# Token rows ahead of conditioning weights in the opening of a hybrid diffusion layer

## The reference

```python
def mixer_layer(x, mod, rms_g, w_in, b_in, ..., attend):
    shift, scale, gate = jnp.split(mod, 3, axis=-1)
    h = rmsnorm(x, rms_g) * (1 + scale) + shift
    q, k, v, z_a, glu, z_b, gates = jnp.split(h @ w_in + b_in, PROJ_SPLITS, axis=-1)
    ...
    return x + gate * (m @ w_out), k, v

mod_ctx = jax.nn.silu(c_ctx) @ w_ada[l] + b_ada[l]
mod_lat = (jax.nn.silu(c) @ w_ada[l] + b_ada[l])[:, None, :]
```

## Time and profile before

| | us |
|---|---|
| median of 3 runs | 1874.98 (1872.67 to 1877.26) |
| the profiled execution | 1877.82 |
| its span, first to last instruction | 1875.6 |
| TensorE busy | 1829.8 (98%) |
| VectorE busy | 1015.1 (54%) |
| ScalarE busy | 542.0 (29%) |
| GpSimd busy | 122.8 (7%) |

### The profile page before, as it was taken

One profiled execution on the slowest core, in us unless ns is written; L12 is line 12 of the kernel. 1 busy time (PEld: TensorE's weight loads), 2 busy tenths in 40 slices (PEclk: granted clock), 3 DMA queues, 4 the chain that ended last, 5 costly groups with the idle time before them and its releaser, 6 DMA issues.

```text
span 1875.6 us, 27263 instructions
## 1 busy us (share of the span) xinstructions
PE 1829.8 (98%) x10723; PEld 1561.1 (83%) x10723; DVE 1015.1 (54%) x1710; ACT 542.0 (29%) x1061; POOL 122.8 (7%) x205
## 2 busy tenths in 40 slices
PE   6999999999999999999999999999999899999998
PEld 3788899988888888888888888888888888888886
DVE  3544512111098338816870996766768555654444
ACT  3731101021111111211110114667768222322221
POOL 0100000000000000000000004322330000000000
PEclk9999999999999999999999999999999999999999
DMA  9524423143022112211220164997887767653321
GB/s 318 169 89 158 144 68 132 49 140 115 12 78 89 65 34 82 76 40 59 72 80 20 65 153 119 211 178 163 175 182 176 229 205 244 193 191 140 141 101 56
DMA packets 211145, 235.08 MB, mean 125 GB/s; under 512 B 47707, under 2 KB 157131, under 8 KB 207819
## 3 DMA queue, kind: packets, MB, share of 16 engines
q1 hardware_dynamic: 210760, 233.24, 42.5%
q10 hardware_dynamic: 259, 0.11, 0.0%
HBM read 152.52 MB, written 80.78 MB: 124 GB/s over the span
## 4 chain that ended last, share of the span: by engine, by line
PE 90%; SPq 4%; DMA 2%; issue 1%; ACT 1%; DVE 1%; POOLq 0%; DVEq 0%; POOL 0%; ACTq 0%
PE banks L789 17%; PE banks L790 17%; PE banks L791 17%; PE banks L1742 4%; PE banks L1741 4%; PE banks L1743 4%; PE banks L1713 3%; PE banks L1715 3%; PE banks L1714 3%; PE banks L1225 3%; SPq L1093 2%; PE banks L784 2%; PE banks L785 2%; PE banks L786 2%; PE banks L1191 2%
## 5 line engine op out<-in xcount | busy, mean ns | idle before, releaser
L789 PE MATMUL banks<-h_hi,w_hi 128*128 128x512 f32 (+1 forms) x1600 | 593.3, 371 | 3.6 <-DVE h_lo L598 2.5
L790 PE MATMUL banks<-h_lo,w_hi 128*128 128x512 f32 (+1 forms) x1600 | 589.4, 368 | 0.0
L791 PE MATMUL banks<-h_hi,w_lo 128*128 128x512 f32 (+1 forms) x1600 | 589.3, 368 | 0.0
L730 DVE SCALAR_TENSOR_TENSOR conv_acc<-glu_out,taps,conv_acc 128x773 f32<-128x773 f32 x360 | 371.5, 1032 | 12.3
L789 PEld LDWEIGHTS banks<-h_hi,w_hi 128*128 128x128 f32 x1600 | 301.8, 189 | 57.6 <-issue 3.4
L791 PEld LDWEIGHTS banks<-h_hi,w_lo 128*128 128x128 f32 x1600 | 301.8, 189 | 50.7
L790 PEld LDWEIGHTS banks<-h_lo,w_hi 128*128 128x128 f32 x1600 | 302.0, 189 | 49.0
L506 ACT ACTIVATE out_stage<-banks,param_cols 128x512 f32<-128x512 f32 (+1 forms) x120 | 77.0, 647 | 439.2 <-PE banks L791 433.2
L1713 PE MATMUL banks<-y_hi,wp_hi 128*128 128x512 f32 (+1 forms) x320 | 120.0, 375 | 4.9 <-DVE m_sum L1935 2.8
L1332 ACT ACTIVATE probs<-scores,stat 128x640 f32<-128x640 f32 (+2 forms) x128 | 106.7, 834 | 60.2 <-DVE stat L1259 58.6
L1715 PE MATMUL banks<-y_hi,wp_lo 128*128 128x512 f32 (+1 forms) x320 | 118.4, 370 | 0.0
(11 more groups left out here) (161 smaller groups left out, 2397.5 us busy)
## 6 DMA issues: line engine op xcount, KB each, us to landing
proj<-out_stage SPq DMA_DIRECT2D x96, 256.0 KB, 2.0
w_raw<-in_w_in SPq DMA_DIRECT2D x44, 512.0 KB, 3.9
gates_in<-proj SPq DMA_DIRECT2D x64, 256.0 KB, 2.9
k_hi<-k_hi_rows SPq DMA_DIRECT2D x16, 640.0 KB, 13.2
k_lo<-k_lo_rows SPq DMA_DIRECT2D x16, 640.0 KB, 15.2
w_ada<-in_w_ada SPq DMA_DIRECT2D x8, 1024.0 KB, 10.8
x_out<-in_x_sample SPq DMA_DIRECT2D x16, 512.0 KB, 3.4
out_y_sample<-x_out SPq DMA_DIRECT2D x15, 512.0 KB, 2.6
```

Source lines behind the costliest of these rows:

```text
L730: op = dve.scalar_tensor_tensor(dst, src, tap, dst, ALU.mult, ALU.add)
L789: pe.matmul(out, w_hi[:, s, k], h_hi[c][:, k], start=first, stop=False)
L790: pe.matmul(out, w_hi[:, s, k], h_lo[c][:, k], start=False, stop=False)
L791: op = pe.matmul(out, w_lo[:, s, k], h_hi[c][:, k], start=False, stop=last)
```

## The change

The rows of chunk 0 are loaded ahead of the first conditioning quarter and in two halves, each `w_in` block ahead of the next quarter, and every engine's written order up to `turn(9)` is changed. The first half of chunk 0 is signalled by `vb_in`, a semaphore that a later load uses too, whose wait becomes 32. `RMS` has one entry more, since the four tiles of chunk 0 are now two pairs.

```diff
-RMS = [(0, 0, 4), (1, 0, 2), (1, 2, 2), (2, 0, 4), (4, 0, 2), (3, 0, 4)]
+RMS = [(0, 0, 2), (0, 2, 2), (1, 0, 2), (1, 2, 2), (2, 0, 4), (4, 0, 2), (3, 0, 4)]
...
-            if c == 1:
-                sp.dma_start(xs[c][:, 0:2], src[:, 0:2]).then_inc(x_half_in, 16)
+            if c < 2:
+                sp.dma_start(xs[c][:, 0:2], src[:, 0:2]).then_inc(x_half_in[c], 16)
...
+        load_x(0)
         load_ada(0)
-        load_x(0)
+        load_w(sp, 0)
         load_ada(1)
-        load_w(sp, 0)
+        load_w(sp, 1)
         load_ada(2)
-        load_w(sp, 1)
+        load_w(sp, 2)
         load_ada(3)
-        load_w(sp, 2)
         load_x(1)
...
+        squares(0, 0)
+        squares(0, 1)
         row_of(0)
-        squares(0)
         high(0)
+        modulate(0)
+        modulate(1)
+        high(1)
         row_of(1)
-        for s in range(4):
-            modulate(s)
-        high(1)
+        modulate(2)
+        modulate(3)
+        high(2)
         row_of(2)
         modulate(4)
         modulate(5)
         row_of(3)
-        high(2)
         squares(1, 0)
         modulate(6)
         modulate(7)
...
+        normalize(0)
+        normalize(1)
         coefficients(0)
-        normalize(0)
         low(0)
+        split(0)
+        split(1)
+        low(1)
         coefficients(1)
-        for s in range(4):
-            split(s)
-        low(1)
+        split(2)
+        split(3)
+        low(2)
         coefficients(2)
         split(4)
         split(5)
-        low(2)
         coefficients(3)
...
-        ada_products(0)
         pe.wait_ge(rows_in, 16 * 7)
         pe.transpose(ps_rows, rows[0:R_C, :], cst.ident[0:R_C, 0:R_C]).then_inc(turned, 1)
         pe.transpose(ps_taps, taps[0:4 * TAPS, :], cst.ident[0:4 * TAPS, 0:4 * TAPS]).then_inc(turned, 1)
-        turn_row(0)
         pe.wait_ge(cols_out, 2)
-        ada_products(1)
         for s in range(3):
             turn(s)
-        turn_row(1)
+        ada_products(0)
+        turn_row(0)
         step(0, [0])
         turn(3)
         step(1, [0])
         turn(4)
+        ada_products(1)
+        turn_row(1)
+        step(0, [1])
+        step(1, [1])
         step(2, [0])
         turn(5)
         step(3, [0])
+        turn(6)
+        step(2, [1])
+        step(3, [1])
         ada_products(2)
-        for s in range(4):
-            step(s, [1])
+        for s in range(3):
+            step(s, [2])
         turn_row(2)
+        step(3, [2])
+        step(4, [0])
+        turn(7)
+        step(4, [1])
         ada_products(3)
-        turn(6)
-        step(4, [0, 1])
+        step(4, [2])
         turn_row(3)
-        turn(7)
-        step(5, [0, 1])
-        for s in range(6):
-            step(s, [2])
+        step(5, [0])
+        turn(8)
+        step(5, [1, 2])
         step(6, [0, 1])
-        turn(8)
+        turn(9)
         step(6, [2])
-        turn(9)
         step(7, [0, 1])
```

More of the change, by code:

```diff
@@ L248, in modulation @@
     ident_in, rows_in, c_in, x_in = sem("ident_in"), sem("rows_in"), sem("c_in"), [sem(f"x_in{c}") for c in range(5)]
-    x_half_in, wide_set = sem("x_half_in"), sem("wide_set")
+    wide_set = sem("wide_set")
     ada_in, gate_in, gb_in, vb_in = [sem(f"weights_in{i}") for i in range(8)], sem("gate_in"), [sem("gate_bias_in0"), sem("gate_bias_in1")], sem("vb_in")
+    x_half_in = [vb_in, sem("x_half_in")]
     tab_zero, tab_in, tab_out = sem("tab_zero"), sem("tab_in"), sem("tab_out")
@@ L447, in squares @@
         def squares(c, half=None):
-            act.wait_ge(x_half_in if half == 0 else x_in[c], 16)
+            act.wait_ge(x_half_in[c] if half == 0 else x_in[c], 16)
             for t in range(CHUNKS[c][1] // P) if half is None else range(2 * half, 2 * half + 2):
@@ L614, in front_dve @@
         split(7)
-        normalize(1)
         normalize(2)
+        normalize(3)
         s = KC
@@ L624, in front_dve @@
             if i == 10:
-                normalize(3)
+                normalize(4)
             if i == 16:
-                normalize(4)
+                normalize(5)
             if i == 19:
-                normalize(5)
+                normalize(6)
         pending = []
@@ L659, in front_dve @@
                 if n == 7 and c == 0:
-                    dve.wait_ge(vb_in, 16)
+                    dve.wait_ge(vb_in, 32)
                 s = slot_of[u]
```

## The result

The changed kernel takes 1890.6 us, median of four runs (1889.6 to 1891.7), before 1875.8 beside them: a ratio of 1.0081 (95% interval 1.0064 to 1.0099), 14.8 us slower. The forecast was 1887, in a range of 1882 to 1892.

A forecast was written before the change was run, and what follows sets the result against it. TensorE was taken as the bound, so an opening shift carries to the end: -4.6 + 2.7 + 3.5 + 7.0 + 3.4 = +12.0 us on the median of 1875.0, forecast 1887 us, range 1882 to 1892.

The forecast's parts named there:

- T0: Start of TensorE's first triple (three products of one k step, one column block): forecast at 26.7 us, 4.6 us earlier.
- (b): TensorE: quarter 1's products and folding, formerly ahead of the first triple, now stand behind its start: +2.7 us.
- (e): TensorE's clock: three restarts at half speed after idle time against one before: +3.4 us, bounds 0 and +6.
- (c): TensorE waits for coefficients around quarter 1's folding, step 2 and step 4: 0.71, 1.04 and 1.73 us, sum +3.5.
- (d): Chunk 1's first turn on TensorE waits 7.2 us, as ScalarE's squares stand behind the copy of quarter 3's sums: +7.0 us.
- rule on the clock: Transposes don't count as busy for TensorE's clock, so the restart at chunk 1 stays slow longer: up to 1 us more.
- No wait in which it could be absorbed, and on to the end: TensorE behind the opening: busy 880.00 of 880.00 us from 120 to 1000 us, so any opening shift reaches the end.
- R1: Rival: the head start wins, no wait at chunk 1's turn on TensorE; 1875 us, not slower; chance 4%.
- R3: Rival: chunk 0's halves or parameter rows arrive late, the first triple stays near 30 us; 1890.3 us; chance 10%.
- R2: Rival: mechanism as forecast, but no further stretch of TensorE at half clock; 1883.6 us; chance 14%.
- R4: Rival: the change doesn't do what it says, for instance loads served in another order; same time, 1875 us; chance 2%.

The follow-up runs named there:

- e1: The changed kernel with ScalarE's squares of chunk 1 ahead of the copy of quarter 3's sums, and VectorE's normalizing of chunk 1 ahead of coefficients(3); 1880.3 us, ratio 1.0027.
- e8: The changed kernel with SyncE's load order of the kernel before, chunk 0 still in halves, all other orders as changed; 1895.3 us, ratio 1.0111.
- e3: The changed kernel with 26 idle TensorE products in front of chunk 1's first turn; 1882.6 us, ratio 1.0041.
- e7: The changed kernel with 50 idle transposes of the identity on TensorE in front of chunk 1's first turn; 1882.7 us, ratio 1.0043.
- e11: The kernel before with 59 idle TensorE products, a delay of 13.6 us, behind the whole opening; 1890.7 us, ratio 1.0079.
- e2: The changed kernel with chunk 1's first turn moved back behind four more triples on TensorE, the next turn behind step 6; 1885.35 us, ratio 1.0049.
- e9: The kernel before with 13 idle TensorE products, a delay of 3.0 us, behind the whole opening; 1874.75 us, ratio 0.9994.
- e5: The kernel before with 22, 25 and 8 idle products in TensorE's three idle stretches of the opening; 1876.2 us, ratio 1.0003.
- e6: The changed kernel's loads with TensorE's order from quarter 2 on laid out anew and idle products in the waits; 1876.0 us, ratio 1.0000.

## Why the prediction was right, point by point

- **T0.** 26.7 forecast, 26.16 measured: -5.1 in place of -4.6. In part this is luck, for several errors cancel. Chunk 0's halves released ScalarE at 7.08 and 9.99, earlier than the 8.6 and 11.1 worked out. Of these 1.1 us the turns got half (15.83 for 16.4), since VectorE came to normalizing only at 12.95, behind the copies of the parameter rows (TensorE began to turn those at 11.85, after its wait of 8.2 us), a place that I had passed over. From the start of the turns to the products it took 2.72 in place of 2.2, the products 3.19 in place of 3.64, and from the folding to VectorE's coefficients 1.09 in place of 0.95.
- **(b) Quarter 1 behind T0.** As forecast, +2.7 at full clock; it ran partly at half clock (2.22), which (e) holds.
- **(c) Waits for coefficients.** Forecast 0.71, 1.04, 1.73; measured 0.73, 0.94, 1.65: 3.3 for 3.5.
- **(d) The turn of chunk 1.** Wait forecast 7.2, measured 6.88, +6.7 for +7.0. e1 shows that ScalarE's order makes it, e8 that no landing does. This was the step on which the sign hung.
- **(e) Clock.** The term that was too small: +3.4 forecast. The stretches at 0.50 hold 5.13, 3.33 and 5.35 us of work, so 6.9 us are lost against 1.7 before: +5.2. The number of restarts was right; the first and the third were longer than the 3.4 us of the earlier trace rows. e3 and e7 take the third away and win 2.5 each. The third cost 1.0 us more than a stretch of 3.4 us would have, the size of the "up to 1 us more" in the prediction's rule on the clock; but its reason, that turns don't count, is what e7 speaks against. The term is that of one pair of executions: e11's opening shows the kernel before without its half clock behind the first triple, and e2 a first stretch of 3.4 us. That the error of this term left the total inside the range is luck in part.
- Sum by the measured terms: -5.1 + 2.7 + 3.3 + 6.7 + 5.2 = 12.8, of 13.7 at the landmark; 0.9 us is not assigned.
- **What carries it to the end.** "No wait in which it could be absorbed, and on to the end" holds to 1150 us only. The prediction had looked at the waits of 120 to 1000 us only and inferred the rest. For 13.7 us it did no harm: e11 gives the changed kernel's time from the delay alone, so nothing of weight was lost elsewhere. For 3 us it fails (e9 shows it; e5 and e6 agree).
- **The rivals.** R1 would have needed what e1 does to ScalarE's order. Even e1 is not at the time of before: 0.27% above it, by the terms because (b), (c) and two of the three stretches of (e) stay. R3's late start did not come, though its ground was partly there: TensorE waited 8.2 us for the parameter rows, and VectorE's normalizing stood behind them. My estimate of that loss is 0.5 us: GpSimd was done at 13.73 and two tiles take 1.42, so 15.15 in place of 15.68. R2's cheap clock is refuted by the stretches above, and R4 by chunk 0's release at 7.08, ahead of quarter 0.

## What to carry to other kernels

When work is moved on one engine, follow for each wait behind it the chain from its true start: here squares that had their data at hand stood behind a copy that waited for a product moved later, and that chain, 9.4 us long, had lost the work of TensorE that covered it. Earlier data is worth only what the orders of all engines can use. And before hunting for two or three microseconds, put a plain delay of that size into the kernel: if the time doesn't answer to it, as here, a gain of that size can't be shown either.

## What was not expected of the hardware

- 50 float32 transposes in a row (5.6 us) kept TensorE's granted clock at full speed through a wait, as 26 plain float32 products did (e7, e3).
- Idle products in the idle time of the opening brought the clock to full early: quarter 0's products took 1.92 us in e5 where they had taken 3.64, and this was worth nothing at the end of the run.
- The same code ran its first 73 us in 71.1 to 73.5 us in four executions, by the moments at which the first loads landed (TensorE's first conditioning products at 11.47 to 12.21) and at which the clock fell and rose.
- A delay of 3.0 us on the engine that is busy 98% of the time did not lengthen the run (1874.75 against 1875.85), while 10.6 and 13.6 us came through with 12.1 and 14.8.
